# Two macaron-style mixer layers and four mixer branches on one core: the depthwise convolution's running sum is kept in a PSUM bank, and the attention's head values share the one bank that is left

## What is computed

```
def forgetting_attention(q, k, v, f_logit):          # 8 heads of 64, 512 tokens
    c = cumsum(log_sigmoid(f_logit))
    ...
    for blk in range(s // Q_BLOCK):                  # blocks of 128 queries
        sc = q[blk] @ k[:qe].T * scale + (c[q] - c[k]); causal mask
        outs.append(softmax(sc) @ v[:qe])

def conformer_conv(glu_in, conv_w, conv_b, g_conv):  # 512 channels, 31 taps
    a = glu_in[..., :CONV_CH] * sigmoid(glu_in[..., CONV_CH:])
    y = causal_depthwise_conv(a, conv_w) + conv_b
    return silu(rmsnorm(y, g_conv))

def hybrid_mixer(u, w_in, ...):
    z = u @ w_in
    y_attn = forgetting_attention(q, k, v, f_logit + b_f) @ w_attn_out
    y_conv = conformer_conv(z[..., C0:GA0], ...) @ w_conv_out
    merged = sigmoid(z[..., GA0:GC0]) * y_attn + sigmoid(z[..., GC0:]) * y_conv
    return merged @ w_out
```

## Time and profile before

| what | value |
|---|---|
| median of 3 runs | 3627.35 us (3626.93 to 3630.12) |
| the profiled execution, its own time | 3626.65 us |
| its span | 3624.8 us |
| PE / PEld busy | 3381.8 us (93%) / 2652.1 us (73%) |
| DVE busy | 2101.9 us (58%) |
| ACT / POOL busy | 1126.6 us (31%) / 1423.8 us (39%) |
| mean granted TensorE clock | 0.964 |

### The profile page before, as it was taken

How to read it: one execution, slowest core, us unless ns; L and a number is a source line. 1 busy time by engine, 2 the same in 40 slices (tenths; PEclk the granted TensorE clock), 3 DMA queues, 4 the chain that set the end, 5 groups by cost and what they waited for, 6 DMA issues and landing times.

```text
span 3624.8 us, 45199 instructions
## 1 busy us (share of the span) xinstructions
PE 3381.8 (93%) x16266; PEld 2652.1 (73%) x16266; DVE 2101.9 (58%) x2934; ACT 1126.6 (31%) x1842; POOL 1423.8 (39%) x693
## 2 busy tenths in 40 slices
PE   9999989899999999999989999978679989998998
PEld 7888866678887788877667888756566656676776
DVE  4443498774434544339977443478963657475653
ACT  3222234422222322223442222332123653344332
POOL 4444454444444344445444444422123213321342
PEclk9999999899999999999989999989789989999999
DMA  4333331223322332333212332514232212321321
GB/s 121 97 89 95 95 82 48 70 87 98 95 87 89 94 96 88 93 96 81 58 58 88 98 98 84 115 33 119 73 112 70 64 37 74 67 47 48 91 82 53
DMA packets 624669, 296.44 MB, mean 82 GB/s; under 512 B 96941, under 2 KB 620846, under 8 KB 624526
## 3 DMA queue, kind: packets, MB, share of 16 engines
q1 hardware_dynamic: 621262, 290.21, 28.7%
q0 software_dynamic: 1328, 2.62, 0.2%
q10 hardware_dynamic: 1936, 1.71, 0.1%
HBM read 287.65 MB, written 6.84 MB: 81 GB/s over the span
## 4 chain that ended last, share of the span: by engine, by line
PE 76%; DVE 18%; issue 3%; ACT 3%; DVEq 0%; DMA 0%; SPq 0%; POOL 0%; ACTq 0%
PE ps L328 23%; PE ps L319 23%; PE ps L320 22%; DVE Y L1724 3%; PE ps L1060 1%; PE ps L1025 1%; PE ps L1049 1%; PE ps L489 1%; DVE T L2699 1%; DVE SS L421 1%; DVE UL L784 1%; DVE T L793 0%; DVE NM L1074 0%; DVE X L798 0%; DVE UL L412 0%
## 5 line engine op out<-in xcount | busy, mean ns | idle before, releaser
L257 POOL TENSOR_TENSOR WL<-RAW,WH 128x1024 fp32r<-128x1024 f32 (+4 forms) x606 | 1316.9, 2174 | 2157.1 <-ACT WH L279 2157.0
L319 PE MATMUL ps<-UH,WH 128*128 128x512 f32 x3056 | 1235.0, 404 | 90.7 <-DVE UL L784 25.2
L320 PE MATMUL ps<-UL,WH 128*128 128x512 f32 x3056 | 1207.9, 395 | 0.0
L279 ACT ACTIVATE WH<-RAW 128x1024 fp32r<-128x1024 f32 (+4 forms) x605 | 571.0, 944 | 1224.0 <-PE ps L328 1136.0
L328 PE MATMUL ps<-UH,WL 128*128 128x512 f32 x3056 | 770.8, 394 | 4.5 <-POOL WL L257 4.5
L319 PEld LDWEIGHTS ps<-UH,WH 128*128 128x128 f32 x3056 | 583.0, 191 | 255.2 <-issue 50.0
L320 PEld LDWEIGHTS ps<-UL,WH 128*128 128x128 f32 x3056 | 583.1, 191 | 126.9 <-issue 6.6
L328 PEld LDWEIGHTS ps<-UH,WL 128*128 128x128 f32 x3056 | 573.6, 189 | 135.9 <-issue 9.3
L1630 DVE TENSOR_TENSOR T<-ps,R 128x512 f32<-128x512 f32 x88 | 60.9, 692 | 393.4 <-PE ps L328 393.4
L319 PE MATMUL ps<-HH,WH 128*128 128x512 f32 x704 | 279.2, 397 | 0.0
L320 PE MATMUL ps<-HL,WH 128*128 128x512 f32 x704 | 276.9, 393 | 0.0
(11 more groups left out here) (447 smaller groups left out, 3563.9 us busy)
## 6 DMA issues: line engine op xcount, KB each, us to landing
RAW<-w_ff_in SPq DMA_DIRECT2D x176, 512.0 KB, 3.7
RAW<-w_in SPq DMA_DIRECT2D x72, 512.0 KB, 3.7
RAW<-w_ff_out SPq DMA_DIRECT2D x64, 384.0 KB, 3.3
RAW<-w_ff_out SPq DMA_DIRECT2D x64, 320.0 KB, 3.1
RAW<-d_w_in SPq DMA_DIRECT2D x24, 512.0 KB, 3.7
RAW<-b_w_in SPq DMA_DIRECT2D x17, 512.0 KB, 3.6
RAW<-w_out SPq DMA_DIRECT2D x16, 512.0 KB, 4.0
RAW<-w_ple_gate SPq DMA_DIRECT2D x16, 512.0 KB, 4.0
```

Source lines behind the costliest of these rows:

```text
L257: e.tensor_tensor(m.WL[:, s, 0:k, :], m.RAW[:, r, 0:k, :], m.WH[:, s, 0:k, :].bitcast(F32), ALU.subtract).then_inc(m.low_ready.sem, 1)
L279: e.activation(m.WH[:, s, 0:k, :], m.RAW[:, r, 0:k, :], ACT.Copy).then_inc(m.high_ready.sem, 1)
L319: e.matmul(out, m.WH[:, s, c, 0:t.cols], H[:, k0 + c, :], start=(x == 0 and c == 0), stop=False)
L320: e.matmul(out, m.WH[:, s, c, 0:t.cols], L[:, k0 + c, :], start=False, stop=False)
```

## The change

1. The running sum of the DVE taps lives in PSUM bank 7. The first tap writes it, the next 21 read and write it, and the last tap reads it and writes Y in SBUF. Counts and order of the taps are the same.
2. The head values of all pairs go to bank 6 (class OneBankHeads). Before the values of a new pair are written, PE waits for the copy-out of the pair just before it; until now it waited for the pair before that one.
3. For pairs 0 to 2 DVE copies the bank out at the end of its own attention step 6, 10 and 14, one step sooner than before. The last pair's copy stays where it was.

```
+    def value_bank(self, c):
+        return 6 + c % 2
+    def wait_values_left(self, e, h, n):
+        if n == 0 and self.h0 + h // 2 > 1:
+            e.wait_ge(self.m.head_out.sem, self.h0 + h // 2 - 1)
...
-                if n == 0 and self.h0 + h // 2 > 1:
-                    e.wait_ge(m.head_out.sem, self.h0 + h // 2 - 1)
+                self.wait_values_left(e, h, n)
...
-                        mm = e.matmul(m.ps[HD * p:HD * p + HD, 6 + h // 2 % 2, n * P:(n + 1) * P], self.v(h + p, n, j),
+                        mm = e.matmul(m.ps[HD * p:HD * p + HD, self.value_bank(h // 2), n * P:(n + 1) * P], self.v(h + p, n, j),
...
+class OneBankHeads(Heads):
+    def value_bank(self, c):
+        return 6
+    def wait_values_left(self, e, h, n):
+        if n == 0 and self.h0 + h // 2 > 0:
+            e.wait_ge(self.m.head_out.sem, self.h0 + h // 2)
+    def heads_out(self, e, s):
+        if (s + 1) // TT < self.pairs // TT - 1:
+            s += 1
+        elif s // TT < self.pairs // TT - 1:
+            return
+        super().heads_out(e, s)
...
-                        y = Y[:, i, :]
+                        y = m.ps[:, 7, :]
...
-                                e.scalar_tensor_tensor(y, src, wj, y, ALU.mult, ALU.add).then_inc(*v.next())
+                                dst = Y[:, i, :] if j == DVE_TAPS - 1 else y
+                                e.scalar_tensor_tensor(dst, src, wj, y, ALU.mult, ALU.add).then_inc(*v.next())
...
-            att = Heads(m, B, HEADS, q=lambda h, n: head(0, h, slice(n * P, (n + 1) * P)),
+            att = OneBankHeads(m, B, HEADS, q=lambda h, n: head(0, h, slice(n * P, (n + 1) * P)),
```

More of the change, by code:

```diff
@@ L1100, in heads_out @@
         self.freed = (m.head_out.sem, self.h0 + c + 1)
-        self.out(self, e, c, m.ps[:, 6 + c % 2, :])
+        self.out(self, e, c, m.ps[:, self.value_bank(c), :])
     def values(self, e, h, n, x):
```

## The result

The changed kernel takes 3596.77 us (median of 4 runs, 3593.92 to 3600.15), against 3627.35 before (also the median of 4 runs, not of 3 as the table says): a ratio of 0.9917, with a 95% interval of 0.9902 to 0.9932, or 30.6 us less. The forecast was 3601.

What follows compares the result with a forecast made beforehand. DVE, held by POOL, was taken to keep PE waiting beside the Q/K and gate tiles. 6.1 + 6.3 = 12.4 us a layer, 24.8 in both, plus 1 for POOL's sums gave 26 and 3601 us, range 3586 to 3615.

Steps and rivals of the forecast that it cites:

- The mechanism: DVE taps: with both tensors in SBUF a tap waits for the running POOL instruction; with one in the bank it does not.
- The price of a tap: DVE tap in the bank: 0.75 us, bounded by an eviction's 0.68 and the longest old tap's 2.957.
- The rival of a slow bank: Taps: reading and writing one bank costs 2.1 us a tap, giving 3737 us; chance 0.06.
- skill's fixed part: Rule against the change: PSUM operations cost about 65 ns more each, 12 us over 184 taps; prediction said the trace disagrees.
- Q/K tiles: Beside the V, Q and K tiles: 7.7 + 2.0 - 3.6 leaves a gain of 6.1 us a layer, ends 9.7 and 3.
- sum of the port waits: Q/K tiles: preparation and close, operands still in SBUF, wait for POOL some 10 us together; seventh tile evicted at about 507.
- Gate tiles: Beside the gate tiles: five of six exponential waits go, 2.0 + 1.5 us stay; gain 6.3 us a layer, ends 9.8 and 3.
- The shared bank: Head values in one bank: first copy out 6 us before PE asks; extra wait 0, at most 1 us a layer.
- The tail: Layer's end: the 4.74 us wait for DVE's division stays, since POOL's last sum goes at PE's pace.
- the 39 us that DVE cost PE: Both layers: 19.5 us a layer of PE waits and lower clock caused by DVE, the most the change could give back.
- rival "all is given back": Both layers: DVE catches up everywhere, 39 us gained, 3588 us; chance 0.17.
- the second rival: Bank taps cost 1.0 to 1.3 us, or port waits move to divisions, preparation, close; 6 to 12 us gained, 3618; chance 0.12.

Runs made afterwards that it cites:

- experiments 1 and 3: Changed kernel with the running sum back in SBUF: 3622.69 us; changed kernel with taps reading two SBUF tensors, writing the bank, sum not accumulated: 3618.26 us.
- experiment 8: Kernel before the change with POOL's tap sums cut to one column of 512: 3606.70 us, one execution.
- experiment 9: Changed kernel with POOL's tap sums cut to one column of 512: 3585.06 us, ratio 0.9889.
- experiment 5: Changed kernel with the convolution's closes two taps later: 3589.90 us, ratio 0.9904.
- experiment 2: Changed kernel with the head copies back at their old step, still one shared bank: 3623.43 us, ratio 0.9991.
- experiment 7: Changed kernel with the closes two taps later and the last close behind DVE's last attention division: 3582.81 us, ratio 0.9878.
- two further edits: Each on the changed kernel: closes two taps later, 3589.90 us; last convolution close moved behind DVE's last attention division, 3589.31 us.

## Why the prediction was right, point by point

**The mechanism** is shown, from three sides. A tap that reads the sum in the bank takes 746 to 758 ns whatever POOL does. A tap with two SBUF inputs takes up to 2.9 us wherever it writes (experiments 1 and 3). With less of POOL's work the taps of before wait less (experiment 8), though POOL's split of the weights is the larger cause. One reading was loose: the tap begun at 467.21 ends 0.55 us behind WL's end, as all the held ones do, which is less than a tap's length of 0.75.

**The price of a tap** was put at 0.75 and is 0.756; the bound of 0.68 and that of 2.957 were both far. The rival of a slow bank, 2.1 us a tap and 3737 us, is out: reading and writing one bank costs 8 ns more than reading it alone (0.756 against 0.748). The 12 us that were worked out from the skill's fixed part are for 184 taps, but the first 8 read no bank; 176 would be 11.

**Q/K tiles: the term that was mis-sized.** A gain of 6.1 us was predicted. The first gate tile's eviction began 83.68 us behind the first V tile's before and begins 74.24 behind it now: 9.4 us. In layer 1 it is 83.84 against 74.26. I had left 2.4 us of wait and up to 1.2 of lower clock; there are 1.25 and none. The step that failed is the sum of the port waits ("some 10 us together"), all of which was counted as DVE's delay. DVE's timeline in the changed kernel:

```profile
488.85 0.69 DVE L1798 SCALAR_TENSOR_TENSOR QKV<-ps,R 128x512 f32<-128x512 f32 x1 [2.25 <-PE ps L328]
...
491.74 3.30 DVE L1849 TENSOR_TENSOR_SCAN PRE<-ONES,PRE 8x512 f32<-8x512 f32 x1
...
497.98 2.23 DVE L1854 TENSOR_SCALAR CUM<-PRE 8x512 fp32r<-8x512 f32 x2
...
501.73 2.70 DVE L1762 TENSOR_TENSOR Y<-Y,YP 128x512 f32<-128x512 f32 x1
...
506.58 0.68 DVE L1798 SCALAR_TENSOR_TENSOR QKV<-ps,R 128x512 f32<-128x512 f32 x1
```

The operations named are indeed held. Beside the time that each took unheld in the kernel before, these three wait 1.1, 1.4 and 2.0 us (2.20, 0.86 and 0.69 there), and those ahead of 488.85 some 3.2 more: 7.7 us in all, an estimate, and not 10. The earlier trace rows have it that POOL is busy 49.4 of 84 us, 3.2 us of each 5.44 us tile and not 4. And the 3.2 us ahead of 488.85 cost nothing: there DVE had caught up and stood idle for 2.25 us. What counts are 4.5 us. So the eviction of the seventh tile came at 506.58. The first V eviction lies 0.56 us later in this trace than in the one before (438.95, 438.39); counted from it, that is 1.0 us sooner than the 507 I had, and PE asked for the bank 0.5 us later than my 505.

By rows 7.7 + 2.0 - 1.25 = 8.45 us are accounted for. The 2.0 us of lower clock behind the wait of 4.6 us are borne out: beside the changed kernel the starts from 514.08 to 518.80 fall back by 2.1 us, as they come 0.43 us apart instead of 0.23. Most of the last 1 us shows too when the two traces are laid side by side matmul by matmul. At the waits of 0.39, 0.66 and 2.02 us they move apart by 0.63, 0.93 and 2.30 us: each wait costs about 0.25 us more than the idle time that its row shows, 0.8 together, which the sum did not have.

**Gate tiles.** Predicted 6.3 us, measured 15.4 - 9.4 = 6.0 in layer 0. The place was right as well: a wait of 1.89 us ahead of step 13 (predicted 2.0), the close in front of it at 2.54 + 1.67 us, the lower clock behind it, and four of the other five waits of the earlier trace rows gone. The fifth was to go too and did not: of 1.79 us at 551.47 there are 0.83 left, at 539.82. ACT has its exponentials queued behind a tap product that waits for POOL's sum; with the sums cut this wait is gone (experiment 9). In layer 1, which I had taken to be like layer 0, it is 17.2 - 9.6 = 7.6 us, and the 1.5 us that were put on the lower clock are what is missing there (below). That it was the close that kept the 1.89 us is not only argued: moved by two taps, it costs nothing (experiment 5).

**The shared bank.** Priced at 0 to 1 us. The first pair's copy starts at 558.70 and PE wants the bank at 565.86: 6.5 us to spare behind the copy's end (4.4 and 6.5 for the next two pairs), and no row of PE waits for it. The sign of being wrong that I named ("if PE waits at L1066 for a copy") is what experiment 2 makes real, with 9.0 us a layer. The new position of the copy is not a nicety but what makes the shared bank free.

**The tail** stayed at 4.74 us, as said. POOL's sums got shorter (median 1.29 against 1.74 us), but ACT's products and the last sum still go at PE's pace.

**The sum.** 26 us were predicted from 3626.65, and 29.7 came. The two stretches gave 32.6, nearly 8 more than the 24.8 predicted for them. That the total came out closer than its terms is partly luck: the rest of the program happened to take 2.9 us longer. The 1 us put on POOL's sums has no row of its own; no wait of PE in the woven stretch names POOL, in either kernel. Of the 39 us that DVE cost PE, the changed kernel gives back some 32 in the stretches, experiment 7 some 46 (226.17 + 226.35 - 203.28 - 203.30). That is more than the 39 that I called the most that could be had. The 39 left out the tail, which I had counted as fixed, and the 0.25 us beside each wait. The time of the rival "all is given back" (3588) is nearly reached by either of two further edits (3589.90 and 3589.31) and passed by both (3582.81). That DVE would be busy 95 to 110 us less was too much (88.7): divisions, preparation and closes took over 23 us of port waits, as the second rival had it, though few of them on PE's path. More than two thirds are the divisions' (16.0), which have one tensor input, in SBUF.

**The two layers** have the same five waits to 0.1 us and yet differ by 1.3 to 1.6 us in their stretches in both executions of the changed kernel. Laid side by side they part at step 13. Layer 1:

```profile
1780.27 0.70 PE L1032 MATMUL ps<-QKV 64*128 64x256 f32 x4 [1.89 <-ACT S L1123]
...
1781.14 1.04 PE L1056 MATMUL ps<-IDENT,S 128*128 128x128 f32 x8
1782.11 0.88 PE L1066 MATMUL ps<-PT,V 128*64 128x128 f32 x12
```

Layer 0 has 1.44 and 1.54 us in these two groups (at 608.98 and 610.36), and slower low-weight matmuls behind them: 1.5 us together. Behind the same wait of 1.89 us the clock falls in layer 0 and not in layer 1. The other execution parts at the same place, by 1.6 us, of which its tail takes back 0.3.

What stays open: executions of one kernel differ by some us outside the stretch, and I have not found by which rows.

## What to carry to other kernels

In this kernel the following held. When a DVE operation of one shape has a minimum and a maximum far apart, lay its slow cases beside GpSimd's timeline before trusting its mean. If they end with GpSimd's instructions, moving one of the two tensor inputs to PSUM removes the wait; moving only the output does not (for a TENSOR_SCALAR with one input in SBUF it did). The bank has to come from somewhere: find who must now leave a bank sooner, and move that copy up in its engine's queue together with the change, since here the taps' gain of some 27 us hung nearly wholly on it. Then look again for what is still held with operands in SBUF, and move it to where nobody waits behind it; that was worth another 14 us.

## What the runs showed of the hardware that was not expected

- Whether a tap with two tensor inputs writes SBUF or PSUM makes no difference to its waiting for GpSimd, and hardly any to its length: 0.748 us with the bank read and SBUF written, 0.756 with the bank read and written, 0.760 (the median) with two SBUF inputs and the bank written. The first tap (TENSOR_SCALAR, one SBUF input) is otherwise: 0.545 to 2.14 us when it writes SBUF, 0.814 flat when it writes the bank.
- A DVE operation with one tensor input, in SBUF, can be held as well if it is a TENSOR_SCALAR: that of L1843 (8x512) takes 2.49 us, those of L1854 (two of the same shape) 0.86 together before and 2.23 now, and the attention's divisions took 16 us more in all once the taps no longer waited in front of them.
- GpSimd gains from it too: its 32 sums of YP and FUN (128x512 each) went from a median of 1.74 to one of 1.29 us; the shortest took 1.27 before and after.
- The length of a wait does not tell whether TensorE's clock falls behind it. Behind 2.02 us at 503.31 in the kernel before, matmuls went on 0.23 us apart, the upper level; behind 1.79 us at 551.47 the low-weight ones took 3.14 us instead of 2.14; and behind 1.89 us ahead of step 13 of the changed kernel the 8 matmuls of L1056 take 1.44 us in layer 0 and 1.04 in layer 1.
